# A decoder layer on one core: units 1 to 5 of the first FFN turned by VectorE's 32x32 blocks instead of by TensorE

## What is computed

```python
mod = silu(c) @ w_ada + b_ada                  # 9 vectors of 2048: shift, scale, gate x 3
sh1, sc1, g1, sh2, sc2, g2, sh3, sc3, g3 = split(mod, 9)
h = rms_norm(x, norm_ffn1) * (1 + sc1) + sh1
x = x + 0.5 * g1 * ((silu(h @ w1_gate) * (h @ w1_up)) @ w1_down)   # 2048 -> 5632 -> 2048
...                                            # token mixing (MLA and NSA heads), second FFN
return rms_norm(x, norm_final)
```

## Time and profile before

| | us |
|---|---|
| median of 3 runs | 2058.04 |
| lowest and highest | 2054.01, 2058.44 |
| profiled execution | 2057.54 |
| its span | 2055.7 |

### The profile page before, as it was taken

The page is one execution under the profiler, slowest core; times in us unless marked ns, Lnnn a source line. Parts: engine busy times, 40 slices in busy tenths (PEclk is TensorE's granted clock), DMA queues, the critical chain, the costliest instruction groups (busy, mean ns, idle before and its releaser), DMA issues.

```text
span 2055.7 us, 26825 instructions
## 1 busy us (share of the span) xinstructions
PE 2020.5 (98%) x9299; PEld 1602.5 (78%) x9299; DVE 1394.0 (68%) x1852; ACT 876.5 (43%) x1127; POOL 36.6 (2%) x56
## 2 busy tenths in 40 slices
PE   7999999999999999999999999999999999999998
PEld 3668888788888888787787888788888888888886
DVE  3557878877778888896556669677775455545454
ACT  4334434344444333543445644544444444434343
POOL 0000000000000000000005000000000000000000
PEclk9999999999999999999999999999999999999999
DMA  9998988899999889698967148589986777676654
GB/s 338 386 333 307 345 319 302 277 301 279 277 317 327 310 307 345 227 368 283 292 195 246 42 142 305 160 285 287 293 249 196 196 203 204 196 216 198 198 186 134
DMA packets 341269, 533.10 MB, mean 259 GB/s; under 512 B 80825, under 2 KB 95252, under 8 KB 340280
## 3 DMA queue, kind: packets, MB, share of 16 engines
q1 hardware_dynamic: 340280, 527.81, 77.6%
q10 hardware_dynamic: 896, 4.06, 0.5%
HBM read 520.04 MB, written 3.89 MB: 255 GB/s over the span
## 4 chain that ended last, share of the span: by engine, by line
PE 94%; DVE 2%; ACT 1%; issue 1%; DMA 1%; ACTq 0%; SPq 0%; DVEq 0%
PE ps L810 29%; PE ps L812 29%; PE ps L811 29%; PE ps L854 1%; PE ps L839 1%; PE ps L872 1%; DVE ada_acc L1903 1%; PE ps L1332 1%; PE ps L1335 1%; PE ps L1362 1%; PE ps L1057 1%; PE ps L1167 0%; DVE w_lo L1885 0%; ACT w_hi L1456 0%; DMA raw<-in_w_uq_dram 0%
## 5 line engine op out<-in xcount | busy, mean ns | idle before, releaser
L1456 ACT ACTIVATE w_hi<-raw 128x1024 fp32r<-128x1024 f32 (+1 forms) x657 | 689.3, 1054 | 928.3 <-PE ps L812 562.9
L1885 DVE TENSOR_TENSOR w_lo<-raw,w_hi 128x1024 fp32r<-128x1024 f32 (+1 forms) x657 | 796.2, 1220 | 404.1 <-ACT w_hi L1456 399.4
L810 PE MATMUL ps<-w_hi,hT_hi 128*128 128x512 f32 (+1 forms) x1856 | 741.3, 399 | 8.7 <-DVE hT_lo L2020 6.1
L812 PE MATMUL ps<-w_hi,hT_lo 128*128 128x512 f32 (+1 forms) x1856 | 731.7, 394 | 0.0
L811 PE MATMUL ps<-w_lo,hT_hi 128*128 128x512 f32 (+1 forms) x1856 | 731.4, 394 | 0.0
L810 PEld LDWEIGHTS ps<-w_hi,hT_hi 128*128 128x128 f32 x1856 | 349.6, 188 | 103.2 <-issue 9.0
L812 PEld LDWEIGHTS ps<-w_hi,hT_lo 128*128 128x128 f32 x1856 | 349.7, 188 | 83.6
L811 PEld LDWEIGHTS ps<-w_lo,hT_hi 128*128 128x128 f32 x1856 | 350.0, 189 | 80.0 <-issue 0.5
L1903 DVE SCALAR_TENSOR_TENSOR ada_acc<-ada_raw,silu_c,ada_acc 128x512 f32<-128x512 f32 x420 | 315.4, 751 | 8.1
L810 PE MATMUL ps<-w_hi,actT_hi 128*128 128x512 f32 x704 | 280.0, 398 | 0.0
L812 PE MATMUL ps<-w_hi,actT_lo 128*128 128x512 f32 x704 | 279.1, 396 | 0.0
(11 more groups left out here) (235 smaller groups left out, 933.3 us busy)
## 6 DMA issues: line engine op xcount, KB each, us to landing
ada_raw<-in_w_ada_dram SPq DMA_DIRECT2D x224, 512.0 KB, 5.4
raw<-in_w_gate_dram SPq DMA_DIRECT2D x176, 512.0 KB, 4.7
raw<-in_w_up_dram SPq DMA_DIRECT2D x176, 512.0 KB, 4.8
raw<-in_w_down_dram SPq DMA_DIRECT2D x176, 512.0 KB, 5.2
raw<-in_w_in_dram SPq DMA_DIRECT2D x72, 512.0 KB, 5.8
ada_half<-in_w_ada_dram SPq DMA_DIRECT2D x16, 2048.0 KB, 13.6
raw<-in_w_out_dram SPq DMA_DIRECT2D x32, 512.0 KB, 5.7
actT_lo<-norm_tmp SPq DMA_DIRECT2D x240, 32.0 KB, 3.2
```

Of the source, the lines that this page charges most:

```text
L810: pe.matmul(bank, lhs_hi, rhs_hi, start=start, stop=False)
L812: return pe.matmul(bank, lhs_lo, rhs_hi, start=False, stop=stop)
L1456: act.activation(part(U, w_hi, s), part(U, raw, s), ACT.Copy).then_inc(hi_done, 1)
L1885: dve.tensor_tensor(part(U, w_lo, s), part(U, raw, s), part(U, w_hi, s).bitcast(F32), ALU.subtract)\
```

## The change

`BLOCKS_FROM` goes from 6 to 1, so that units 1 to 9 of the first FFN go by blocks. Units up to `LAST_HELD` = 5 are held: their sixteen DMAs are issued ahead of SP's panels 0 to 3 of the second unit behind (and not ahead of panels 12 to 15 of the next), ACT splits them at j = 5 and DVE at j = 6 of that unit. `block_products` stands at j = 6 behind that split in units 2 to 7, since `norm_tmp` is one buffer. PE's transposes of units 1 to 5 are gone, and so is the wait of `turn_redone` for the split of the unit before, whose banks it shared. SP's unit 7 is written out as well, and its loop begins at unit 8.

```diff
-        BLOCKS_FROM, BLOCK_DMAS = 6, 16
+        BLOCKS_FROM, BLOCK_DMAS = 1, 16
+        LAST_HELD = REDO + 3
...
+        def held(f, u):
+
+            return f == 0 and u <= LAST_HELD
+
...
-                    if U.stage in ("gu0", "gu1") and U.first > 0 and by_blocks(int(U.stage[2]), U.first - 1) and j >= 12:
-                        turn_blocks(int(U.stage[2]), before(U), range(4 * (j - 12), 4 * (j - 12) + 4))
+                    f = int(U.stage[2]) if U.stage in ("gu0", "gu1") else None
+                    if f == 0 and U.first > 2 and held(f, U.first - 2) and j < 4:
+                        turn_blocks(f, before(before(U)), range(4 * j, 4 * j + 4))
+                    if f is not None and U.first > 0 and not held(f, U.first - 1) and j >= 12:
+                        turn_blocks(f, before(U), range(4 * (j - 12), 4 * (j - 12) + 4))
...
-            for u in range(REDO, REDO + 5):
+            for u in range(REDO, REDO + 6):
                 load_unit(Unit("gu0", u), gate_up(0))
-            for U in units(sp, "gu0", REDO + 5, STAGES["gu0"][0]):
+            for U in units(sp, "gu0", REDO + 6, STAGES["gu0"][0]):
                 load_unit(U, gate_up(0))
...
             def turn_redone():

                 pe.wait_ge(redo_sum, 3 * TT)
-                pe.wait_ge(gu[0]["actT_lo_done"], 2 * order(0, REDO + 4))
...
                     hi(U, j)
-                    if j == 0 and U.first > 1 and by_blocks(f, U.first - 2):
+                    if U.first > 1 and by_blocks(f, U.first - 2) and j == (5 if held(f, U.first - 2) else 0):
                         actT_of_blocks(f, before(before(U)))
...
                     lo(U, j)
                     if j == 1:
                         product(f, before(U))
-                    if j == 0 and U.first > 1 and by_blocks(f, U.first - 2):
+                    if U.first > 1 and by_blocks(f, U.first - 2) and j == (6 if held(f, U.first - 2) else 0):
                         blocks_low(f, before(before(U)))
-                    if j == 2 and by_blocks(f, U.first - 1):
+                    if by_blocks(f, U.first - 1) and j == (6 if f == 0 and held(f, U.first - 2) else 2):
                         block_products(f, before(U))
```

## The result

The changed kernel takes 2061.9 us (median of 20 runs, 2058.37 to 2065.64), the kernel before 2057.22 in the same comparison (20 runs, 2053.85 to 2059.11). The ratio of the changed kernel's time to that of before is 1.0027, with a 95% interval of 1.0021 to 1.0032: it is slower by 0.27%, about 5 us. The forecast was that it would be faster by 3.6 us. The time lies outside the range of 2049.7 to 2058.6.

What follows compares the result with a forecast made beforehand. The prediction took TensorE (PE), busy 98% of the span, as the bound. 4.3 us off PE less 0.35 for DVE and 0.4 for DMA gave 3.55, say 3.6, so 2057.54 became 2053.9 us; range 2049.7 to 2058.6.

Steps and rivals of the forecast that it cites:

- What leaves PE: First FFN, units 2 to 6: eight PE transposes fewer in each, 4.3 us gained, all on the chain.
- What DVE gets: Units 2 to 6: two block transposes each, hidden except in unit 6, where w_lo 7 comes late: -0.35 us.
- 4 us to spare at w_lo 7: Plain unit: DVE's new order ends w_lo 7 at T+15.7, PE needs it at T+19.7.
- What the DMA queue gets: Units 3 to 7: sixteen 32 KB transfers each on SP, checked for issue, queued loads and engine work; term -0.4 us.
- (a): Issue on SP, units 3 to 7: four transfers and a load take 3.2 us, upper bound 3.55.
- (b): Loads queued behind the transfers: load 1 issued 5.8 us after the last redo load, landing in 4.5 us, in time.
- I take no wait: Start of units: load 1 lands early enough for hi 1 and silu, so PE's panel 0 loses nothing.
- bound of 1 us in each of two units: Upper limit on PE's loss should load 1 land late for hi 1 and silu.
- (c): DMA engines' work: sixteen transfers take 6.3 us of share; unit 5 needs 44.8 of 45.4 us and fits.
- −0.4 for the store in unit 4: ACT's 1.7 MB bias store delays loads 2 to 7, w_lo 7 at 21.0 against 20.55: -0.4 us, bounds 0 and 2.
- Rival 2: DVE and silu eat more through slower landing, issue and late w_lo 7: gain 0.8 to 2.3, about 2056 us; chance 0.20.
- Rival 3: DMA engines become the bound in units 3 to 5: slower, 2059.2 us, or 2065 with second gaps; chance 0.14.

Runs made afterwards that it cites:

- e3: Changed kernel with the transfers of units 1 to 5 on ACT's queue, two behind each hi of panels 8 to 15: 2053.57 us, 0.9982 of before.
- e1: Changed kernel without the transfers of units 1 to 5, whose products stay unturned: 2055.12 us, 0.9989 of before.
- e5: Kernel before plus two unread DVE block transposes at j = 6 in units 2 to 6, PE still turning: 2056.71 us, 0.9999 of before.
- e9: Changed kernel with ACT's silu ahead of hi 1 in units 3 to 6: 2060.60 us, 1.0015 of before.
- e6: Changed kernel with the 1.7 MB bias store issued one unit earlier, after unit 2: 2062.06 us, 1.0023 of before.
- e0: The changed kernel run again as it is: 2060.89 us, 1.0020 of before.
- e10: Changed kernel with the transfers of units 1 to 5 on SP ahead of panels 12 to 15 of the unit behind: 2057.50 us, 1.0004 of before.
- e12: e3 with redo_hi and redo_low two panels later in unit 6, measured in more rounds: 2052.15 us, 0.9980 of before.
- e13: e3 with the transfers four behind each of hi 12 to 15 instead of two behind hi 8 to 15: 2056.46 us, 0.9997 of before.

## Why the prediction was wrong

**What leaves PE, 4.3 us: right.** 0.88, 0.86, 0.86 and 0.87 in units 2 to 5 of e3, where nothing is late.

**What DVE gets, −0.35 in unit 6: right.** 48.82 to 48.95 in e3 and e1, where 48.8 was predicted. The count of DVE's order holds where the loads are in time, also in units 4 and 5 (46.27 and 45.4). e5's 49.36 shows that blocks alone cost nothing there; the −0.35 needs the whole new order. In the changed kernel the count of 4 us to spare at w_lo 7 didn't hold, because it took load 4 to be in time.

**What the DMA queue gets: here it failed, in (a) and (b), and so in "I take no wait".**

- (a) took 3.2 us for four transfers and a load, with 3.55 as the upper bound. Measured from the first of four to the load's end they are 3.94 and 5.27 in front of unit 4, and in front of unit 5 3.28 and 4.3 (282.79 to 286.07, 286.11 to 290.41). The first four take 2.6 us in two of the three units, as reckoned. It is the second four, behind them in the queue, that take 3.7 to 3.9. Of the rows that the price came from the earlier trace rows, the one of the down projection is from a quiet stretch (share 0.06 just before it). The one of unit 8 is not (share 1.01), but it is the first four of its unit, with no redo loads in the queue; the four behind it, at 462.71, took 3.21, which with a load is over the bound of 3.55. So the 5.8 us from the first transfer to load 1 became 7.9, 7.0 and 7.7 in units 4, 5 and 6.
- (b) took 4.5 us for load 1 to land, with the argument that it follows thinner traffic. It took 8.9, 5.8 and 5.4. The row of unit 3 had 8.7 as its highest, in units that were as full; the choice below its median of 6.5 was the mistake. The 8.9 has the bias store beside it: the prediction had this store delay loads by some 4 us, but loads 2 to 7, and it fell on load 1. In unit 4 the load left 9.2 us ahead of the unit (that part of the count was right) and 2.1 of these belong to hi 1 and silu: 8.9 - 7.1 = 1.8, and PE waited 1.58. In unit 6 the issue was late instead, 5.9 ahead of the unit, and PE waited 1.44. "I take no wait" should have been 1.6, 0.2 and 1.4 us.
- The bound of 1 us in each of two units was too low for what was missing altogether: the loads behind load 1 are late as well. w_lo made PE wait 2.6 us, of which 0.7 is old and 0.2 in unit 7. e9 shows that this isn't a separate matter: with silu out of the way it is 4.5.
- (c) put sixteen transfers at 6.3 us of engine time. With them on ACT's queue the view of queues tells them apart from the loads. Queue, packets, MB and share, 301.4 to 347.7 us, before:

```profile
q1 hardware_dynamic: 7627, 14.70, 88.2%
```

and in e3:

```profile
q1 hardware_dynamic: 7909, 15.24, 96.0%
q10 hardware_dynamic: 4352, 0.53, 8.1%
```

  The transfers themselves take 8.1% of 46.3 us, 3.8 us. The loads beside them take 2.92 us per MB instead of 2.78, some 2.1 us more, which makes 5.9 in all. The size was nearly right, and it was no bound. The estimate by the Trainium skill's 78% (DMA: Bandwidth & Descriptors, "Why small descriptors are slow (HBM only)") is 1.7 us; this trace doesn't agree with it, nor did the rows of before.
- The −0.4 for the store in unit 4 was for a wait at w_lo 7 there, and none came (46.27 in e3, which keeps the store at its place). Where the loads leave late, the store costs more, and at load 1 (e6).

**Sum by the profile.** In units 2 to 6, 4.3 us leave PE, and yet they take 1.9 us more than before (0.88 less in unit 2, 2.78 more in units 3 to 6), so 6.2 us were lost. That is 3.3 for silu, 1.7 for w_lo (2.6 less the 0.7 of before and the 0.2 of unit 7), and 1.2 us in smaller pieces. The medians say that a usual execution loses 9 us (4.3 + 4.7). The profiled one is near the fastest. e0's, with 2060.43 near its median, shows 0.7 us more in these units (192.53 against 191.85) and one way to it: the waits are shorter, and the low clock behind one of them costs 1.5 us. How often that comes, and where the rest goes, stays open.

**Rivals.** Rival 2 named the right places, silu behind hi 1 and w_lo, but its price of 2 to 3.5 us had the same low issue time in it. Rival 3 had the sign by another mechanism. What was missing was a rival in which SP's issue slows down under load, and with it the chain from late loads over w_lo 4 to DVE's fuller panel 6. A hint stood in the trace of before, but not in the rows that were read: the four at 462.71 with 3.21 us. The rule of the Trainium skill in VectorE: DVE Perf Modes, "Rules for kernel authors", to transpose 128x128 on TensorE, came out right for this change and wrong for the kernel: with the transfers on ACT's queue the blocks win by 3.7 us (0.9982 of before).

## What to carry to other kernels

An issue time read from the first of several small DMAs is a lower bound: price those behind it by the worst row that the trace has, and every load behind them by the sum. In this kernel small transfers did no harm on the queue that carries no loads, two at a time, beside an instruction of the issuing engine of about their length (1.28 and 1.06 us); four at a time held that engine up. Slack that was counted with all inputs in time says nothing once they are late: a place that had 4 us to spare made PE wait. And a wait of PE can cost more than its length, since a lower clock may follow it. Before a wait is mended at its first reader, look whether the data behind it are late as well; if so, the wait only moves.

## What the hardware showed beyond that

- The first modulation transposes (unit 1) stand between 143.11 and 148.12 us in the profiled executions, though all kernels run the same instructions up to there. This follows no change and is as large as the whole effect; a comparison of stretches has to begin behind it. Windows of 20 to 40 us, before:

```profile
20.00:40.00 20.00, 17.28 (x63) 9.29 (x62) 9.29 (x21) 13.89 (x32) 0.00 (x0) 1.00 1.03 372
```

and in the changed kernel, where the granted clock is lower (0.79 in the mean, of levels 1.2 and 2.4 GHz) and yet unit 1 is reached 3.1 us earlier:

```profile
20.00:40.00 20.00, 17.74 (x78) 9.22 (x81) 11.03 (x23) 12.17 (x26) 0.00 (x0) 0.79 1.05 386
```

  In ten of the sixteen profiled executions the clock is at half for 7 to 10 us between 18 and 30 us, and they reach unit 1 between 143.11 and 146.21; the six in which it stays high there reach it between 146.61 and 148.12. Which of the two follows from the other was not tried.

- From the transposes of unit 10 to the end, the span has 1482.9 to 1483.5 us in ten profiled executions and 1484.5 to 1484.7 in six (the changed kernel, e0, e9, e10, e12, e13). In these six, the granted clock falls in the mean of a window of 5 us between 1290 and 1305 us, at the passage to the second FFN, to 0.66 to 0.80; in the ten it stays at 1.00. It comes with 1.4 us more in the mean, in fast kernels and slow ones (e12 has the best median), so it doesn't go with the waits in the first FFN. Yet none of the four kernels in which PE turns units 1 to 5 has it, and six of the twelve others have, both profiles of the changed kernel among them; whether the change makes it more frequent is open, and so is whether it is a part of the difference of the medians. What brings it about was not tried.
